# Turning activations with VectorE and memory instead of TensorE: h, the low-rank rows, the merged rows, and a dense layout for the feed-forward

## The reference

```python
h = _layernorm(x, ln_emb_g, ln_emb_b)
proj = h @ w_in[l]          # HGRN2 q, i, f_fw, f_bw, g; c_q, c_kv, k_rope; q_mem; three gates
y_hg  = _hgrn2_branch(...)
y_mla = _mla_branch(...)    # _rmsnorm(c_q) @ w_uq, _rmsnorm(c_kv) @ w_ukv, then attention
y_mem = _memory_branch(q_mem, mem, mem_w_kv[l])
merged = sum over b of sigmoid(gate_b) * (y_b @ w_branch[l, b])
h = _layernorm(ALPHA * h + merged @ w_o[l], ln1_g[l], ln1_b[l])
ff = (silu(h @ w_ffn_gate[l]) * (h @ w_ffn_up[l])) @ w_ffn_down[l]
h = _layernorm(ALPHA * h + ff, ln2_g[l], ln2_b[l])
```

## Time and profile before

| what | value |
|---|---|
| median of 3 runs | 1773.02 us (1772.24 to 1776.79) |
| the profiled execution | 1772.84 us |
| its span in the profile | 1771.1 us |
| TensorE busy | 1755.3 us, 99% |
| VectorE, ScalarE busy | 999.6 us (56%), 756.4 us (43%) |
| mean granted clock of TensorE | 0.998 |
| DMA | 366.17 MB, 207 GB/s on the mean |

### The profile page before, as it was taken

The page is one execution under the profiler, slowest core; times in us unless marked ns, Lnnn a source line. Parts: engine busy times, 40 slices in busy tenths (PEclk is TensorE's granted clock), DMA queues, the critical chain, the costliest instruction groups (busy, mean ns, idle before and its releaser), DMA issues.

```text
span 1771.1 us, 19613 instructions
## 1 busy us (share of the span) xinstructions
PE 1755.3 (99%) x8448; PEld 1521.8 (86%) x8448; DVE 999.6 (56%) x874; ACT 756.4 (43%) x655; POOL 85.2 (5%) x77
## 2 busy tenths in 40 slices
PE   9999999999999999999999999999999999999997
PEld 8888888988888888888888888888888888999997
DVE  5865556677766655445656764555555555443445
ACT  4455444454544445444444433433343433333331
POOL 0000002222221200000000000000000000000000
PEclk9999999999999999999999999999999999999999
DMA  9765555444444557656666737777777777755553
GB/s 351 246 235 181 190 189 190 166 167 177 166 162 173 171 199 262 215 181 238 234 238 250 296 102 218 222 217 214 213 215 216 220 220 219 261 182 183 184 188 119
DMA packets 105251, 366.17 MB, mean 207 GB/s; under 512 B 7904, under 2 KB 30816, under 8 KB 87136
## 3 DMA queue, kind: packets, MB, share of 16 engines
q1 hardware_dynamic: 99040, 354.07, 59.1%
q10 hardware_dynamic: 6144, 11.14, 1.7%
HBM read 344.09 MB, written 20.45 MB: 206 GB/s over the span
## 4 chain that ended last, share of the span: by engine, by line
PE 97%; DMA 1%; DVE 1%; ACT 0%; SPq 0%; issue 0%
PE pair L1425 25%; PE pair L1427 25%; PE pair L1426 25%; PE pair L1396 9%; PE pair L1394 5%; PE side L1500 2%; DMA raw<-in_stream 1%; PE pair L1406 1%; PE pair L1407 1%; PE pair L1408 1%; PE pair L1393 1%; PE pair L1378 0%; PE side L1483 0%; PE side L1555 0%; PE side L1533 0%; PE side L1556 0%
## 5 line engine op out<-in xcount | busy, mean ns | idle before, releaser
L903 DVE TENSOR_TENSOR weight_lo<-raw,weight_hi 128x2048 fp32r<-128x2048 f32 x293 | 672.4, 2296 | 618.5 <-ACT weight_hi L602 617.1
L602 ACT ACTIVATE weight_hi<-raw 128x2048 fp32r<-128x2048 f32 x293 | 561.5, 1916 | 852.7 <-DMA raw<-in_stream 852.5
L1425 PE MATMUL pair<-weight_hi,act_both 128*128 128x512 f32 x1312 | 516.6, 394 | 0.9 <-DVE weight_lo L903 0.9
L1427 PE MATMUL pair<-weight_hi,act_both 128*128 128x512 f32 x1312 | 510.9, 389 | 0.0
L1426 PE MATMUL pair<-weight_lo,act_both 128*128 128x512 f32 x1312 | 510.6, 389 | 0.0
L1427 PEld LDWEIGHTS pair<-weight_hi,act_both 128*128 128x128 f32 x1312 | 246.3, 188 | 51.8
L1425 PEld LDWEIGHTS pair<-weight_hi,act_both 128*128 128x128 f32 x1312 | 246.4, 188 | 51.6 <-issue 1.6
L1426 PEld LDWEIGHTS pair<-weight_lo,act_both 128*128 128x128 f32 x1312 | 246.5, 188 | 50.3 <-issue 0.2
L1396 PE MATMUL pair<-act_both,weight_hi 128*128 128x512 f32 x600 | 211.3, 394 | 0.0
L1394 PE MATMUL pair<-act_both,weight_lo 128*128 128x256 f32 x640 | 172.8, 280 | 0.0
L1427 PE MATMUL pair<-weight_hi,ff_lo 128*128 128x512 f32 x352 | 139.9, 398 | 0.0
(11 more groups left out here) (230 smaller groups left out, 1562.5 us busy)
## 6 DMA issues: line engine op xcount, KB each, us to landing
raw<-in_stream SPq DMA_DIRECT2D x294, 1024.0 KB, 5.0
scratch<-spill ACTq DMA_DIRECT2D x40, 256.0 KB, 4.2
ln_rows<-in_ln_rows SPq DMA_DIRECT2D x6, 1024.0 KB, 7.8
gate<-scratch SPq DMA_DIRECT2D x12, 512.0 KB, 5.9
ff_scratch<-ff_blocks SPq DMA_DIRECT2D x11, 512.0 KB, 3.6
ff_raw<-ff_scratch SPq DMA_DIRECT2D x44, 128.0 KB, 6.4
extra_raw<-in_stream SPq DMA_DIRECT2D x4, 1024.0 KB, 9.5
raw<-in_stream SPq DMA_DIRECT2D x4, 512.0 KB, 8.9
```

What stands on the lines that cost most here:

```text
L602: act.activation(hi_of(n), raw_of(n), ACT.Copy).then_inc(extra_h if extra(n) else h_ready, 1)
L903: dve.tensor_tensor(lo_of(n), raw_of(n), hi_of(n).bitcast(F32), ALU.subtract)\
L1425: pe.matmul(out, hi[still], w_hi[:, k, :], start=first and k == 0, stop=False)
L1427: mm = pe.matmul(out, lo[still], w_hi[:, k, :], start=False, stop=last and k == 3)
```

## The change

All turned rows but those of the second layer norm now go the way of the feed-forward, and the layout changes: the stepped read moves from the matmul to ScalarE and VectorE, which read a landing buffer (`h_land`, `c_land`, `merged_land`, `ff_land`) with a step of four floats and write hi and lo dense over tokens.
- h: VectorE turns the squares in slots 10 to 13, SP saves and fetches them between loads 15 and 20 in two buffers, ScalarE rounds in slots 14 to 17, VectorE subtracts in slots 15 to 18, and TensorE waits for one quarter (`h_lo`) before each piece of c_q. The fetches 2 and 3 wait until `h_lo` says that their buffer is free.
- c_q, c_kv: squares in slots 22 and 26, saves after loads 27 and 31, fetches after loads 29 and 33, hi in slots 30 and 34, lo in slots 31 and 35.
- merged: chunks 0 to 2; chunk 3 stays on TensorE.
- feed-forward: one landing buffer in place of eleven; each fetch waits for the subtraction of the one before (`ff_l`).

The core of the diff:

```diff
+            def fetch(u, land, done):
+                for m in range(QUADS):
+                    src = turned_scratch[u, TT * m:TT * m + TT].rearrange("t (i a) e -> a (t i) e", i=QUADS)
+                    sp.dma_start(land[SQ * m:SQ * m + SQ].rearrange("p (s e) -> p s e", e=P), src).then_inc(done, 16)
...
+            def fetch_h(c):
+                sp.wait_ge(h_out, 16 * (c + 1))
+                if c >= 2:
+                    sp.wait_ge(h_lo, c - 1)
+                fetch(c, h_land[:, c % 2], h_in)
...
-            loads(12, 20)
+            for n in range(12, 20):
+                load(Nth(n))
+                if 16 <= n:
+                    fetch_h(n - 16)
+                if 15 <= n < 19:
+                    save_h(n - 15)
             sp.wait_ge(h_done, 8)
...
+                if k in (5, 8, 11):
+                    save_merged(k // 3 - 1)
+                if k in (6, 9):
+                    fetch_merged(k // 3 - 2)
...
-            sp.wait_ge(merged_l, 8)
+            sp.wait_ge(merged_l, 5)
...
+                if H_SLOT <= n < H_SLOT + 4:
+                    c = n - H_SLOT
+                    act.wait_ge(h_in, 16 * QUADS * (c + 1))
+                    act.activation(act_hi[:, 4 * c:4 * c + 4, :], h_land[:, c % 2].rearrange("p (t k) -> p k t", k=4),
+                                   ACT.Copy).then_inc(h_hi, 1)
...
+                if NORM_SLOT + 2 <= n < NORM_SLOT + 6:
...
+                    for t in range(TT):
+                        squares(h_blocks[:, c % 2], t, h_tok[:, t, c * 512:(c + 1) * 512], h_blocked)
+                if H_SLOT < n <= H_SLOT + 4:
+                    c = n - H_SLOT - 1
+                    dve.wait_ge(h_hi, c + 1)
...
-                        if hi is ff_hi:
-                            still = (slice(None), k0 // 4, slice(t * P * 4 + k, (t + 1) * P * 4, 4))
-                        else:
-                            still = (slice(None), k0 + k, slice(t * P, (t + 1) * P))
...
+                        tok = slice(t * P, (t + 1) * P)
+                        pe.matmul(out, hi[:, k0 + k, tok], w_hi[:, k, :], start=first and k == 0, stop=False)
...
-                if LN_SLOT <= n < LN_SLOT + 4:
-                    for b in (2 * (n - LN_SLOT), 2 * (n - LN_SLOT) + 1):
-                        turn(b, h_tok, 0, h_done)
...
-            pe.wait_ge(turned_l, 8)
-            t_phase("c_q", 4, 4, act_hi, act_lo)
+            pe.wait_ge(ident_in, 16)
+            for j in range(4):
+                pe.wait_ge(h_lo, j + 1)
+                t_piece(Nth(FIRST["c_q"] + j), GROUP["c_q"], j, 4, act_hi, act_lo)
```

More of the change, by code:

```diff
@@ L297, in encoder_program @@
         c_scaled = sem("c_scaled")
-        c_turned = sem("c_turned")
+        c_blocked = sem("c_blocked")
+        c_out = sem("c_out")
+        c_in = sem("c_in")
+        h_blocked = sem("h_blocked")
+        h_out = sem("h_out")
+        h_in = sem("h_in")
+        h_hi = sem("h_hi")
+        h_lo = sem("h_lo")
         c_hi_done = sem("c_hi_done")
@@ L472, in _ @@
                 sp.dma_start(h_scratch[t * P:(t + 1) * P, :], h_tok[:, t, :]).then_inc(h_saved, 16)
-            loads(20, HG_END + 1)
+            for n in range(20, 36):
+                load(Nth(n))
+                if n in (27, 31):
+                    save_c((n - 27) // 4)
+                if n in (29, 33):
+                    fetch_c((n - 29) // 4)
+            loads(36, HG_END + 1)
             sp.wait_ge(hg_mult, hg_count(PAIRS - 1, 9) + 1)
@@ L489, in _, with save_merged, fetch_merged @@
             loads(HG_END + 13, first)
+            def save_merged(c):
+                sp.wait_ge(m_blocked, c + 1)
+                sp.dma_start(merged_scratch[c].rearrange("m p e -> p m e"), merged_blocks[:]).then_inc(m_out, 16)
+            def fetch_merged(c):
+                sp.wait_ge(m_out, 16 * (c + 1))
+                if c == 2:
+                    sp.wait_ge(merged_l, 1)
+                for m in range(QUADS):
+                    src = merged_scratch[c, TT * m:TT * m + TT].rearrange("t (i a) e -> a (t i) e", i=QUADS)
+                    dst = merged_land[SQ * m:SQ * m + SQ, c % 2].rearrange("p (s e) -> p s e", e=P)
+                    sp.dma_start(dst, src).then_inc(m_in, 16)
             for k in range(12):
@@ L503, in _ @@
                     .then_inc(gate_full[k % 3], 16)
+                if k in (5, 8, 11):
+                    save_merged(k // 3 - 1)
+                if k in (6, 9):
+                    fetch_merged(k // 3 - 2)
             first = FIRST["w_o"]
-            loads(first, first + 4)
-            sp.wait_ge(merged_l, 8)
+            load(Nth(first))
+            fetch_merged(2)
+            loads(first + 1, first + 4)
+            sp.wait_ge(merged_l, 5)
             sp.wait_ge(h_saved, 32)
@@ L947, in lo_of_turned, with squares @@
                    .then_inc(turned_l, 1)
+            def squares(blocks, t, rows, done):
+                dst = blocks.rearrange("p (m t) (b k) -> p t k m b", t=TT, k=4)[:, t]
+                ins = dve.transpose(dst, rows.rearrange("p (k m b) -> p k m b", k=4, m=QUADS))
+                if t == TT - 1:
+                    ins.then_inc(done, 1)
             def lower_bounds(first):
@@ L1209, in _, with block_merged, lo_of_turned_merged @@
             g0 = GROUP["branch"]
-            def lo_of_merged(c):
+            def block_merged(c):
+                dve.wait_ge(merged_sum, c + 1)
+                if c:
+                    dve.wait_ge(m_out, 16 * c)
+                for t in range(TT):
+                    squares(merged_blocks[:], t, merged[:, c % 2, t, :], m_blocked)
+            def lo_of_merged(c):
+                dve.wait_ge(merged_h, c + 1)
+                part = (slice(None), slice(4 * c, 4 * c + 4))
+                dve.tensor_tensor(act_lo[part], merged_land[:, c % 2].rearrange("p (t k) -> p k t", k=4),
+                                  act_hi[part].bitcast(F32), ALU.subtract)\
+                   .then_inc(merged_l, 1)
+            def lo_of_turned_merged():
                 for t in range(TT):
-                    dve.wait_ge(merged_h, 2 * c + t + 1)
-                    hi = act_hi[:, 4 * c:4 * c + 4, t * P:(t + 1) * P]
-                    dve.tensor_tensor(act_lo[:, 4 * c:4 * c + 4, t * P:(t + 1) * P],
-                                      side[(2 * c + t) % 4][:].rearrange("p (k t) -> p k t", k=4), hi.bitcast(F32),
+                    dve.wait_ge(merged_h, 4 + t)
+                    hi, lo = (a[:, 12:16, t * P:(t + 1) * P] for a in (act_hi, act_lo))
+                    dve.tensor_tensor(lo, side[2 + t][:].rearrange("p (k t) -> p k t", k=4), hi.bitcast(F32),
                                       ALU.subtract).then_inc(merged_l, 1)
@@ L1420, in tokens @@
                     for k in range(4):
[L1421 to L1427 removed]
+                        tok = slice(t * P, (t + 1) * P)
+                        pe.matmul(out, hi[:, k0 + k, tok], w_hi[:, k, :], start=first and k == 0, stop=False)
+                        pe.matmul(out, hi[:, k0 + k, tok], w_lo[:, k, :], start=False, stop=False)
+                        mm = pe.matmul(out, lo[:, k0 + k, tok], w_hi[:, k, :], start=False, stop=last and k == 3)
                 return mm
```

137 lines of the change are left out of this document (75 added, 62 removed).

## The result

The changed kernel takes 1780.63 us, median of 5 runs (1779.17 to 1783.16); the kernel before, on the same chip, 1773.02 us (1772.24 to 1776.79). The ratio is 1.0043, with an interval from 1.003 to 1.0055. So the change costs 7.6 us, a little more than a measurement of this kernel can tell from no change. The forecast was 1777.3 us, with a range of 1770 to 1786. It is right in its range and in its mechanism, and 3.3 us low.

The account below looks back on a forecast made before the run. TensorE, busy 1755.3 of 1771.1 us, was taken to bound the kernel, so its waits count in full. Sum: 1772.84 - 8.8 - 1.8 - 2.7 + 0.3 + 15.5 + 2 = 1777.3 us, range 1770 to 1786.

Parts of the forecast that it names:

- Down, -8.8: Down projection: dense ff_hi and ff_lo bring matmul distance from 0.2350 to 0.2267 us over 1056 matmuls, -8.8 us.
- c turns, -1.8: Low-rank rows (c_q, c_kv): two groups of eight turns leave TensorE, 0.89 us each, -1.8 us.
- Merged turns, -2.7: Merged rows: three of four groups of turns leave TensorE, -2.7 us.
- w_o, +0.3: Output stage w_o: z's wait for merged_l holds load 4 behind one more subtraction, +0.3 us, bounds 0 and 1.2.
- c_q stage, +15.5: c_q: TensorE waits for late h_lo, losing 10.6 to 17.6 us, first layer norm's turns already given back; taken +15.5.
- clock, +2: Behind piece 19 of c_q: clock at half speed after idle time, +2 us, bounded by nothing and 5.4 us.
- 3.6 for the turns: First layer norm: four groups of turns leave TensorE, -3.6 us, counted inside the c_q sum.
- The subtraction of h, 1.2 us: VectorE's subtraction making each h_lo in c_q, priced at 1.2 us.
- The rival of two pieces at half speed: Behind the wait before piece 19: two pieces at half speed, 10.9 us instead of 2, 1786.2 us; 12 in 100.
- Hidden chain: c_q rival: h_lo come before pieces 16 to 19 are due, all four groups gained, 1755.9 us; 8 in 100.
- Slower by the clock: Rival behind piece 19's wait: clock stays at 1.2 GHz for two pieces, 1786.2 us; 12 in 100.
- the dense layout gives nothing: Down-stage rival: something else causes the 0.2350 us, so the -8.8 is missing, 1786.1 us; 5 in 100.

Follow-up runs that it names:

- experiment 1: The kernel before with only the dense layout of ff_hi and ff_lo and one feed-forward landing buffer: 1764.6 us, ratio 0.995.
- experiment 2: The changed kernel with h turned by TensorE as before; c, merged and the feed-forward keep the detour: 1765.37 us, ratio 0.9956.
- experiment 5: Experiment 2 with SP's wait for merged_l moved from the first z transfer to load 12 of w_o: 1762.65 us, ratio 0.9946.
- experiment 7: Experiment 1 with the c_q and c_kv rows by the detour, h and merged on TensorE: 1764.07 us, ratio 0.995.
- experiment 8: The changed kernel run again with no edit: 1780.68 us, ratio 1.0036.
- experiment 9: The changed kernel with only SP's wait for merged_l moved from the first z transfers to load 12 of w_o: 1778.91 us, ratio 1.0028.
- experiment 3: The changed kernel with h's subtraction ahead of the weights' lo half in VectorE's slots 15 to 18: 1765.39 us, ratio 0.9969.
- experiment 6: The changed kernel with the edits of experiments 3, 4 and 5 together, and bounds and angles in slots 20 and 22: 1763.19 us, ratio 0.9939.
- experiment 10: The changed kernel with only bounds and angles moved from slots 16 and 18 to 20 and 22: 1776.72 us, ratio 1.0015.
- experiment 4: The changed kernel with the two 1 MB saves of h_tok behind load 23 instead of ahead of load 20: 1773.83 us, ratio 1.0006.

## Why the prediction was right, and what was off

**Sum.** 1777.3 forecast, 1780.6 measured, and each term can be held against a place of the trace.

- *Down, -8.8.* Right: the stage takes 239.1 instead of 247.9 us from its first matmul to its last, in the changed kernel and in experiment 1; by the times of experiment 1 it is 8.2.
- *c turns, -1.8.* The shift falls from 18.4 to 16.6 between c_q and the attention. Right in this profile, which has no wait for q_nope; experiments 2, 5 and 7 show that 0.7 us or more of it can go back into one (1.27, 1.6 and 1.22 us, where experiment 1 has 0.50). The times don't resolve it.
- *Merged turns, -2.7.* The shift is 2.3 us less at w_o's turns than at the attention (14.3 and 16.6), 0.36 us of waiting for the sum included. Right. But the sum can be 2.13 us late in another execution (experiment 8), which the forecast had no term for: it asked about the loads of the branch stage and not about the instruction that VectorE must do last.
- *w_o, +0.3.* Undersized. It measured 1.7 in the profile (the shift grows from 14.3 to 16.0; 1.29 of it is the wait before piece 4). The medians of experiments 9 and 5, 1.8 and 2.7 us less without SP's wait, fit but aren't resolved by their spread. The mechanism was the one named, and its upper bound, 1.2, was too low. The first transfer of z goes out 7.5 us after chunk 3's turns begin (967.03 and 959.56), before it was 5.1 (950.39 and 945.28): 2.4 us later, of which the added subtraction is 2.0 and was taken at 1.2. Less the slack of 0.9 that the forecast read, that is 1.5 us; 1.29 stand in the trace. SP's wait for this subtraction was 9.9 us before; SP's waits in the changed kernel have it so:

```profile
SPq L593 <- DVE act_both L1345: 12.8, 1, 12.8
```

- *c_q stage, +15.5, and clock, +2.* Together +16.2 measured (18.4 less the 2.2 that were there at 68.5). The steps, in the trace's time, which is 2.2 us late: waits of 0.90 and 1.17 before pieces 13 and 14 (forecast 1.0 and 1.7); piece 17 starts at 115.67 (111.1 to 116.0); load 20 is issued at 118.50 (113.9 to 118.8) and landed at 128.9 (123.7 to 130.6); the last `h_lo` is done at 136.0 (129.9 to 136.9). The idle times are 4.76 and 6.28 us; 5 and 8 were forecast. Less the 2.2, each lies in its bounds. The brackets sum to 14.1, but they count from the modelled end of the matmul before, 0.39 us after its start, where the next would have started after 0.2267; each is 0.16 us or more short. From start to start it is 1.2 and 1.4 us before pieces 13 and 14, 1.3 before 16, 4.9 before 17 and 6.4 before 19, and 3.0 and 1.5 us for the matmuls at half speed behind the last two: 19.7, less 3.6 for the turns 16.1.
- *The subtraction of h, 1.2 us.* Wrong as a size: 2.0 us. The forecast moved the stepped read from TensorE to two other engines and priced it there at nothing, though the very rows that carry the -8.8 said that such a read is slow. In c_q it cost less than it could, because the landing of load 20 came out at 10.4 us where up to 11.8 had been allowed.
- *The clock.* +2 was about right: behind piece 19's start 1.5 in the first profile, 2.8 in the second. Behind piece 17's it was 3.0, and the wait before piece 19 is shorter by it, as the forecast had it. The Trainium skill (TensorE: Matmul & The Clock Gate, Part 1: The HAM clock gate) says of the start of a kernel that the stretch at the low clock varies from run to run; the restarts here, in the middle of one, do the same, with 2.9 and 5.6 us at 1.2 GHz after waits of 6.28 and 6.43 us. The rival of two pieces at half speed, 10.9 us, is out.

The 3.3 us between forecast and measurement are thus the early wait (+2.2 in the profiled execution), the w_o term (+1.4), the longer wait at the start of ffn (+0.5) and the merged turns (+0.4), less 1.3 that c_q and the clock together came out below their 17.5. So the forecast is as near as it is in part by luck: errors of both signs, and one cause that it did not have. The early wait is the landing time of one load near 39 us (experiment 8), and why it is long in the three profiles of kernels that are the changed one up to w_o, and in none of the other nine, stays open.

**Rivals.** Hidden chain: out in the kernel as changed, but not by much of an edit; in experiment 3 it is hidden but for 4 us, in experiment 6 from piece 15 on altogether. There is nothing in the detour itself that costs 15 us. *Slower by the clock* and *the dense layout gives nothing*: both out, as above.

## What to carry to other kernels

When a step is moved from the bounding engine to engines with time to spare, their free share (44% and 58% busy here) says nothing; write out each queue between the producer and the consumer, and ask for every instruction what it stands behind. Here a 2 us subtraction stood behind 4 us of angles and behind the halves of a weight that was needed later; moving it ahead of the lo half of its slot, in experiment 3, gave back 15.2 us. A wait in a DMA queue should stand at the transfer whose buffer it protects (experiments 5 and 9: waits of 2.25 and 1.29 us on TensorE gone), and a change that bundles a sure gain (the dense layout, 8.2 us) with a doubtful one should be measured apart: with every obstacle that was found cleared, the detours added some 2 us to it.

## What the runs showed of the hardware that I had not expected

- A read with a step of four floats costs on each of the three engines that do it here. TensorE's weight load: 310 ns, dense 188. ScalarE's copy of 128x1024 into ff_hi: 2.07 us, 1.04 in the kernel before. VectorE's subtraction: 2.01 us, 1.22 before. Moving it off the bounding engine is right; it isn't free where it goes.
- A load of 1 MB issued behind four fetches with rows of 512 bytes and two saves of 1 MB lands in 10.4 us, and in 12.1 us in experiment 10, against 5.4 us at the median. Behind the four fetches alone it lands in 5.2 us (experiment 4).
- The time until the clock is back hardly goes by the length of the wait. Nine times it fell in c_q behind a wait of 3.80 to 6.43 us, and it was back 2.7 to 6.1 us into the work: after 6.1 us behind a wait of 4.76, after 2.9 behind 6.28, after 5.6 behind 6.43. Nor does the fall itself: it fell behind 2.25 us (experiment 2, w_o) and 2.06 us (experiment 10, ffn), and not behind 3.15 us (experiment 3) or 2.21 us (experiment 4, before piece 16). A single profile doesn't price a wait of several microseconds to better than some 1.5 us.
